# Dense products whose results nobody reads, issued by TensorE inside a sparse attention core: 12 at its beginning, 6 at the second and third query block, one at the other scores

## The reference, cut to what matters

```python
def one_block(bi):                       # one of 4 query blocks of 128
    dots = jnp.einsum('bqhd,bsd->bqhs', iqb, ikf) * IDX_DIM ** -0.5
    score = jnp.einsum('bqh,bqhs->bqs', iwb, jax.nn.relu(dots))
    _, sel = lax.top_k(score, k_top)     # the 128 best keys of each query
    ...
    bias = rel_table[rel_bucket(posq[:, :, None] - take_rows(positions, sel))]
    logits = jnp.einsum('bqhd,bqkd->bqhk', qb, k_sel) * A_HEAD_DIM ** -0.5
    logits = logits + jnp.swapaxes(bias, 2, 3)
    p = jax.nn.softmax(logits, axis=-1)
    return jnp.einsum('bqhk,bqkd->bqhd', p, v_sel)
```

## Time and profile before

| | us |
|---|---|
| median of 3 runs | 2277.66 |
| the profiled execution, by the host's measure | 2286.9 |
| its span, first to last instruction | 2285.1 |
| TensorE busy in the span | 2150.5 (94%) |
| VectorE busy in the span | 1339.0 (59%) |
| mean granted TensorE clock | 0.943 |
| the stage `dsa` in the span | 1697.4 to 1823.3 |

### The profile page before, as it was taken

One profiled execution on the slowest core, in us unless ns is written; L12 is line 12 of the kernel. 1 busy time (PEld: TensorE's weight loads), 2 busy tenths in 40 slices (PEclk: granted clock), 3 DMA queues, 4 the chain that ended last, 5 costly groups with the idle time before them and its releaser, 6 DMA issues.

```text
span 2285.1 us, 26165 instructions
## 1 busy us (share of the span) xinstructions
PE 2150.5 (94%) x10612; PEld 1701.3 (74%) x10614; DVE 1339.0 (59%) x2273; ACT 875.1 (38%) x1453; POOL 146.2 (6%) x96
## 2 busy tenths in 40 slices
PE   6999889999998999889999998999889999999998
PEld 5755778888887866677888887777555588888886
DVE  5697468847844466547743654468766564633532
ACT  3455434423422255524432433223553433422421
POOL 0463100000010000010000001000000001000000
PEclk9999879999998999979999998999885999999999
DMA  7443225565531220112333222222100032333331
GB/s 270 139 151 97 65 65 192 186 211 166 180 96 49 83 65 29 33 42 79 101 97 97 92 88 66 83 75 65 38 27 1 2 96 80 101 102 92 101 93 65
DMA packets 61752, 214.80 MB, mean 94 GB/s; under 512 B 6848, under 2 KB 7744, under 8 KB 61632
## 3 DMA queue, kind: packets, MB, share of 16 engines
q1 hardware_dynamic: 61632, 213.12, 29.4%
HBM read 211.00 MB, written 2.10 MB: 93 GB/s over the span
## 4 chain that ended last, share of the span: by engine, by line
PE 87%; DVE 7%; ACT 3%; issue 2%; POOL 1%; DMA 0%; SPq 0%; POOLq 0%; DVEq 0%; ACTq 0%
PE bank L285 23%; PE bank L287 23%; PE bank L286 23%; PE bank L290 16%; PE bank L752 2%; DVE wlo L325 1%; DVE steps L805 1%; ACT whi L312 1%; ACT pr L725 1%; DVE tmp L488 0%; DVE Hl L493 0%; DVE sc L1861 0%; POOL small L468 0%; DVE steps L1859 0%; DVE pr L717 0%
## 5 line engine op out<-in xcount | busy, mean ns | idle before, releaser
L285 PE MATMUL bank<-Hh,whi 128*128 128x512 f32 x1632 | 656.5, 402 | 54.9 <-DVE wlo L325 8.4
L287 PE MATMUL bank<-Hh,wlo 128*128 128x512 f32 x1632 | 646.9, 396 | 0.0
L286 PE MATMUL bank<-Hl,whi 128*128 128x512 f32 x1632 | 646.7, 396 | 0.0
L325 DVE TENSOR_TENSOR wlo<-stg,whi 128x1024 fp32r<-128x1024 f32 (+1 forms) x299 | 358.9, 1205 | 438.6 <-ACT whi L312 438.0
L312 ACT ACTIVATE whi<-stg 128x1024 fp32r<-128x1024 f32 (+1 forms) x309 | 314.0, 1026 | 441.5 <-PE bank L287 437.7
L285 PEld LDWEIGHTS bank<-Hh,whi 128*128 128x128 f32 x1632 | 313.6, 192 | 129.2 <-issue 14.2
L287 PEld LDWEIGHTS bank<-Hh,wlo 128*128 128x128 f32 x1632 | 313.2, 192 | 67.7
L286 PEld LDWEIGHTS bank<-Hl,whi 128*128 128x128 f32 x1632 | 314.0, 192 | 62.8 <-issue 0.2
L287 PE MATMUL bank<-HIDh,wlo 128*128 128x512 f32 x352 | 140.4, 399 | 0.0
L286 PE MATMUL bank<-HIDl,whi 128*128 128x512 f32 x352 | 138.7, 394 | 0.0
L285 PE MATMUL bank<-HIDh,whi 128*128 128x512 f32 x352 | 138.0, 392 | 0.0
(11 more groups left out here) (284 smaller groups left out, 2725.6 us busy)
## 6 DMA issues: line engine op xcount, KB each, us to landing
raw<-in_mod_w SPq DMA_DIRECT2D x96, 512.0 KB, 4.2
stg<-in_ffn_in SPq DMA_DIRECT2D x88, 512.0 KB, 4.2
stg<-in_ff SPq DMA_DIRECT2D x64, 512.0 KB, 3.6
stg<-in_ffn_out SPq DMA_DIRECT2D x40, 512.0 KB, 3.6
stg<-in_cm_w SPq DMA_DIRECT2D x24, 512.0 KB, 3.8
stg<-in_gates SPq DMA_DIRECT2D x16, 512.0 KB, 3.5
stg<-in_z_ch SPq DMA_DIRECT2D x12, 512.0 KB, 3.7
stg<-in_w_k SPq DMA_DIRECT2D x8, 512.0 KB, 3.6
```

Of the source, the lines that this page charges most:

```text
L285: pe.e.matmul(out_, l[0], r[0], start=start, stop=False, skip_group_check=True)
L286: pe.e.matmul(out_, l[0], r[1], start=False, stop=False, skip_group_check=True)
L287: return pe.e.matmul(out_, l[1], r[0], start=False, stop=stop, skip_group_check=True)
L325: hand.e.tensor_tensor(wlo[j % NW][:, 0:n * c], stg[j % NSTG][:, 0:n * c], whi[j % NW][:, 0:n * c].bitcast(F32), ALU.subtract).then_inc(*m ...
```

## The change

A helper `fill(n, b)` issues n products of 128x128 weights over 512 columns, both operands from `YBh[:, 0]`, into score bank b of the item that comes next. Nobody reads the results: the mask product of the item starts the bank anew. Before them it takes the same wait that the scores would take for that bank, and one for `YBh`. TensorE's `lead_dsa` calls it ahead of everything else of the iteration: 12 products at item 0, 6 at items 8 and 16, one at every other item up to 23, none in the last block. The calls of `lead_dsa` for VectorE and ScalarE are as before.

```diff
-            def lead_dsa(biases):
+
+            def fill(n, b):
+                for m, step in left.get(b, ()):
+                    pe.wait_ge(*m[step])
+                pe.wait_ge(*act_done["ybh", 0])
+                for _ in range(n):
+                    mm(banks[b][:, :], YBh[:, 0, 0:P], YBh[:, 0, :], True, True)
+
+            def lead_dsa(biases, filled=None):
                 now = {}
 
                 def lead(i):
                     qb = i // 8
+                    if filled and qb < 3:
+                        fill({0: 12}.get(i, 6 if i % 8 == 0 else 1), dsa.score_bank(i, 0))
                     if i == 0:
                         all_of(biases(0))
...
-                all_of(dsa.tensor(None, lead_dsa(lambda qb: steps_pe("ds", 4 * FIRST[qb], 4 * (FIRST[qb + 1] - FIRST[qb]), Tb, [4, 5]))))
+                all_of(dsa.tensor(None, lead_dsa(lambda qb: steps_pe("ds", 4 * FIRST[qb], 4 * (FIRST[qb + 1] - FIRST[qb]), Tb, [4, 5]), True)))
```

## The result

The changed kernel takes 2297.78 us (median of 4 runs, 2294.59 to 2300.86) against 2278.16 (4 runs) for the kernel before. The ratio is 1.0079, 95% interval 1.0065 to 1.0094: 18 us slower, or 15 to 21. The forecast was 2280.2 us in a range that ended at 2290. Its sign was right, but its +2.5 us lay inside the 4.6 us that it could not tell from none, so the sign is no merit; the size was wrong. It went as the second rival said (2288.7 us), and beyond it.

What follows compares the result with a forecast made beforehand. The prediction took TensorE, at half clock, to set the sparse core's pace. Products costing 9.5 us less 7 us regained from the clock gave +2.5 us, 2277.66 to 2280.2 us, in a range of 2267 to 2290.

Steps and rivals of the forecast that it cites:

- the second rival: Sparse core: products cost 12.5 us at half clock, only 1.5 regained; +11 us, 2288.7 us; chance 0.30.
- TensorE sets the pace, at half clock: Sparse core: TensorE busy 17.60 of 17.70 us in block 0, 31.32 of 34.30 in block 1, at clock 0.50.
- The 12 at the start cost nothing and put the first fall off by one item: Item 0: 12 products, 2.66 us, fit the 2.68 us idle time, cost 0; the clock falls one item later.
- The gaps at 9, 13, 17 and 21 keep 1.2 us or more: TensorE's waits at these items: one 0.22 us product shortens each from 1.75 to 1.53 us; 1.2 or more stays.
- Of 45 products 29 are on TensorE's path: Sparse core: 12 at the start and 4 in gaps are covered, leaving 29 products on TensorE's path.
- They cost 29 x 0.33 = 9.5 us: The 29 products on TensorE's path, priced at a mean of the full-clock and half-clock prices: 9.5 us.
- The clock gives 7 us back: Sparse core: 7 of 16.9 us regained, 2 in block 0, 2 around item 8, 3 from item 16 on.
- 35 to 55 us at half clock: Sparse core: expected sum of half-clock time after the change, down from 71.6 us.
- The sign that was to tell the whole: Start of the `w_branch_a` products, 1823.3 before: 1825.8 by the forecast, 1810 with clock full, 1834 by the second rival.
- If the clock were full throughout, 13 us faster: Rival, chance 0.14: full clock through the core gives 16.9 us, less net product cost 3.9; 13 us faster, 2264.7.
- 1.35 us at six items: Query block 1: full clock saves 1.35 us at six items, nothing at the two with a gap; put at 7.6 us.
- block 2's 17.0 us by block 1's ratio: Query block 2: of 17.0 us of half clock, a third, by block 1's ratio, would be saved: 5.3 us.

Runs made afterwards that it cites:

- only_first: Changed kernel with only the 12 dense products at item 0, none later; ratio to the kernel before 0.9999.
- only_bursts: Changed kernel with only the six dense products at items 8 and 16, none elsewhere; ratio to the kernel before 1.0021.
- more_singles: Changed kernel with 12 products at item 0 and three instead of one at every other item of query blocks 0 to 2; ratio to the kernel before 1.0007.
- in_gaps: Changed kernel with six dense products at each of items 9, 13, 17 and 21, none elsewhere; ratio to the kernel before 0.9955.
- only_singles: Changed kernel with only the single dense products at the 21 items between, none at items 0, 8 and 16; ratio to the kernel before 1.0051.
- narrow_in_gaps: Changed kernel with six products at items 9, 13, 17 and 21 only, cut to 32 rows and 32 weight columns; ratio to the kernel before 0.9999.
- first_and_gaps: Changed kernel with 12 dense products at item 0 and six at items 9, 13, 17 and 21, none elsewhere; ratio to the kernel before 0.9946.

## Why the prediction was wrong, point by point

- *TensorE sets the pace, at half clock; the gaps stand at items 9, 13, 17, 21; the bursts come one item ahead of them.* Right, and this decided the case.
- *The 12 at the start cost nothing and put the first fall off by one item.* Right: 1.00 in 1697.60:1702.20, down at 1703.3, and only_first is at 0.9999.
- *The gaps at 9, 13, 17 and 21 keep 1.2 us or more.* Half right: 0.77 and 0.56 us at items 9 and 13, where the single ran at half clock, 1.32 and 1.31 at 17 and 21.
- *Of 45 products 29 are on TensorE's path.* The count holds; the singles in the gaps are covered (0.56 to 1.32 us of idle time is left of 1.28 to 1.75).
- *They cost 29 x 0.33 = 9.5 us.* Mis-sized. A lone product at half clock costs 0.59 us, not 0.43, and most ran at half clock. In items 1 to 8 seven of them and a burst make 0.34 + 6 x 0.59 + 2.73 = 6.6 us; measured +6.4. Of the 17 singles on the path 14 ran at half clock and 3 at full, of the bursts one each: 14 x 0.59 + 3 x 0.34 + 2.73 + 1.50 = 13.5 us for the 29.
- *The clock gives 7 us back.* This step failed most: it gave nothing. The core grew by 14.1 us, all of the products' 13.5 and a little more. I took 35 to 55 us at half clock; it was 78.5, and over the runs the whole program has 259 us where before has 246. Block 0 regained nothing: the fall came 1 us into the first scores and no single lifted it. The burst at item 8 did not bring the clock up at all here (0.60 in 1725.80:1761.70, up only at 1754.5), and in only_bursts it did and lost it in the gap 3.4 us later. Items 13 to 15 gave some 2 us back (items 8 to 15 grew by 1.8 where their products cost 4), and items 16 to 23 lost them again: they grew by 5.9 where their products cost 2.7, with 27.3 us at half clock where there had been 17.9.
- *The second rival* (12.5 less 1.5) had the mechanism; its price was low by the lone product's 0.16 us, and it let the clock give something back. Its chance of 0.30 was too small beside 0.48 for a forecast that needed the bursts to work, against my own reading that they stood in the wrong place. The sign that was to tell the whole, the start of `w_branch_a`, came out at 1834.88 beside this rival's 1834; in part that is luck, since the core also began 2.5 us earlier in this profile (1694.87 against 1697.38).
- *If the clock were full throughout, 13 us faster.* Its working has a slip: 1.35 us at six items is 8.1, not 7.6, and block 2's 17.0 us by block 1's ratio (1.36 of 4.10) give 5.6, not 5.3. The size holds all the same: more_singles gave some 15 to 17 us for nearly full clock, where I had 16.9 ahead of the products' price. in_gaps gained 10.3 us with fewer products and still 23.9 us at half clock. The step that the changed kernel would not get there was right.
- Open: of the 18 us by the runs the core's profiles show 14 to 17. The rest is not attributed. That only_singles has more half clock than the changed kernel (92.2 us against 78.5) is one launch each; over the runs they are level, 261 and 259 us, and both lie 13 to 15 us above before. The products' own time at half clock, 16 x 0.59 = 9.4 us and 14 x 0.59 + 2.73 = 11.0, would make most of that; why one product an item does not lift the clock and three do, no run here settles. Nor was a burst in the first gap alone tried.

The page of the Trainium skill that I weighed, "TensorE: Matmul & The Clock Gate", section "Why this matters for your kernels", wants TensorE busy continuously. narrow_in_gaps kept it busy for 118.64 of its core's 123.9 us at a mean clock of 0.75, in_gaps for 107.12 of 112.7 us at 0.89: at a like busy share the size of the products decided, so the rule alone does not tell these two apart.

## What to carry to other kernels

Filler work belongs in the wait itself, at the instruction that stands still: the same 45 products lost 18 us with their two bursts one item ahead of a gap and nothing with the bursts in it, and 24 products in the four gaps, none elsewhere, gained 10. Price a filler by what it does to the next start in its own surroundings, not by its rate in a long run of its kind, and count the ones that no wait covers before hoping for the clock. To test whether the clock or the filled wait brings a gain, shrink the product to a corner of the array and keep its length.

## What the runs showed of the hardware that I had not expected

- A lone 128x128 by 512 product in fp32r ahead of bf16 products delays them by 0.59 us at half clock and 0.34 at full, where such products in a row start 0.43 and 0.22 us apart; in bf16, with other data, it was 0.40 at half.
- The clock does not follow the time that TensorE is busy: six products of 32x32 weights in each gap left 61.4 us of half clock, six of 128x128 left 23.9, over the same 512 columns at the same places (in the whole program, over the runs, 241 and 209 us).
- Once up in item 9, the clock of in_gaps stayed at full for the remaining 84 us of a core that had spent half its time below it, with 18 more dense products (three gaps of six); first_and_gaps had one fall of 3.4 us there.
